# Reading the half-exchanged queries and keys of a rotary embedding by permuted row transfers in place of products with a permutation matrix

## The reference, cut to what matters

```
def rotate(xp, pos):
    half = xp.shape[-1] // 2
    ...
    x1, x2 = jnp.split(xp.astype(jnp.float32), 2, axis=-1)
    return jnp.concatenate([x1 * cos - x2 * sin, x1 * sin + x2 * cos], axis=-1)
rd = HEAD_DIM // 2
return jnp.concatenate([rotate(x[..., :rd], row), rotate(x[..., rd:], col)], axis=-1)
```

## Time and profile before

| | us |
|---|---|
| median of 3 runs | 3360.63 |
| lowest, highest | 3359.15, 3364.89 |
| span of the profiled execution | 3357.8 |
| busy: TensorE, its weight loads | 3114.1 (93%), 2493.0 (74%) |
| busy: VectorE, ScalarE, GpSimd | 1500.2, 1162.7, 831.6 |

### The profile page before, as it was taken

One profiled execution on the slowest core, in us unless ns is written; L12 is line 12 of the kernel. 1 busy time (PEld: TensorE's weight loads), 2 busy tenths in 40 slices (PEclk: granted clock), 3 DMA queues, 4 the chain that ended last, 5 costly groups with the idle time before them and its releaser, 6 DMA issues.

```text
span 3357.8 us, 79208 instructions
## 1 busy us (share of the span) xinstructions
PE 3114.1 (93%) x34382; PEld 2493.0 (74%) x34382; DVE 1500.2 (45%) x2358; ACT 1162.7 (35%) x2403; POOL 831.6 (25%) x518
## 2 busy tenths in 40 slices
PE   7999898999999998999999888989899989989998
PEld 5777676778777786888888666767667667768886
DVE  4455473745444653100144464756565456330033
ACT  4433333423334424211112353434333345342222
POOL 2211111111123132222223221111111243434453
PEclk9999999999999999999999989999999999999999
DMA  5424242434454441111111233413233343522222
GB/s 212 135 97 145 81 142 101 130 121 144 145 166 151 158 169 57 51 63 62 62 50 63 75 101 98 127 63 120 65 122 106 93 140 115 188 69 95 99 88 75
DMA packets 246714, 364.56 MB, mean 109 GB/s; under 512 B 154080, under 2 KB 155376, under 8 KB 245904
## 3 DMA queue, kind: packets, MB, share of 16 engines
q1 hardware_dynamic: 226976, 294.57, 27.6%
q10 hardware_dynamic: 14976, 35.66, 2.7%
q0 software_dynamic: 4464, 29.92, 2.5%
HBM read 290.88 MB, written 69.21 MB: 107 GB/s over the span
## 4 chain that ended last, share of the span: by engine, by line
PE 76%; DVE 6%; issue 5%; ACT 4%; DMA 2%; DVEq 2%; POOLq 2%; PEld 1%; SPq 1%; POOL 0%; PEldq 0%; ACTq 0%
PE banks L281 20%; PE banks L282 18%; PE banks L283 18%; PE banks L1684 2%; PE banks L1023 2%; PE banks L1695 1%; PE banks L1648 1%; PE banks L395 1%; PE banks L1687 1%; PE banks L1745 1%; POOLq L2430 1%; DVE arena L597 1%; PE banks L2057 1%; PE banks L1051 1%; DMA arena<-chunk_inputs 1%
## 5 line engine op out<-in xcount | busy, mean ns | idle before, releaser
L283 PE MATMUL banks<-hx_rounded,slot_rounded 128*128 128x512 f32 (+1 forms) x1624 | 575.1, 354 | 0.0
L906 POOL TENSOR_TENSOR slot_rounded<-slot,branch_weights_high 128x512 fp32r<-128x512 f32 x188 | 251.4, 1357 | 1286.2 <-ACT branch_weights_high L901 1284.9
L281 PE MATMUL banks<-hx_high,weight_parts 128*128 128x512 f32 (+1 forms) x1512 | 537.9, 356 | 10.9 <-DVE hx_low L545 10.4
L281 PE MATMUL banks<-hx_rounded,branch_weights_high 128*128 128x512 f32 (+1 forms) x1280 | 498.8, 390 | 48.1 <-DVE arena L1364 8.6
L282 PE MATMUL banks<-hx_low,weight_parts 128*128 128x512 f32 (+1 forms) x1512 | 538.0, 356 | 0.0
L283 PE MATMUL banks<-hx_high,weight_parts 128*128 128x512 f32 (+1 forms) x1512 | 535.9, 354 | 0.0
L282 PE MATMUL banks<-resid_rounded,branch_weights_high 128*128 128x512 f32 (+1 forms) x1280 | 452.7, 354 | 0.0
L283 PEld LDWEIGHTS banks<-hx_rounded,slot_rounded 128*128 128x128 f32 x1624 | 312.2, 192 | 44.3
L281 PEld LDWEIGHTS banks<-hx_rounded,branch_weights_high 128*128 128x128 f32 x1280 | 245.9, 192 | 128.2 <-issue 75.6
L281 PEld LDWEIGHTS banks<-hx_high,weight_parts 128*128 128x128 f32 x1512 | 286.6, 190 | 55.1 <-issue 14.3
L283 PEld LDWEIGHTS banks<-hx_high,weight_parts 128*128 128x128 f32 x1512 | 286.3, 189 | 41.1
(11 more groups left out here) (263 smaller groups left out, 5853.7 us busy)
## 6 DMA issues: line engine op xcount, KB each, us to landing
slot<-in_w_mix SPq DMA_DIRECT2D x120, 512.0 KB, 3.9
slot<-in_w_ffn_in SPq DMA_DIRECT2D x88, 512.0 KB, 3.3
arena<-chunk_inputs SPq DMA_DIRECT2D x48, 640.0 KB, 4.5
arena<-in_w_ada SPq DMA_DIRECT2D x50, 512.0 KB, 5.1
slot<-in_w_ffn_out SPq DMA_DIRECT2D x44, 512.0 KB, 3.3
slot<-in_w_ada SPq DMA_DIRECT2D x40, 512.0 KB, 4.3
chunk_inputs<-arena SPq DMA_DIRECT2D x80, 256.0 KB, 3.9
arena<-side_projections POOLq DMA_DIRECT2D x16, 1152.0 KB, 6.1
```

Source lines behind the costliest of these rows:

```text
L281: first = nc.tensor.matmul(out, w_hi, x_hi, start=start, stop=False)
L283: return first, nc.tensor.matmul(out, w_lo, x_hi, start=False, stop=stop)
L906: last = nc.gpsimd.tensor_tensor(slots_r[g % 3][:, half], slots[g % 3][:, half], weights_high(g)[:, half], ALU.subtract)
```

## The change

The two products with PERM are taken out. The exchanged queries and keys are read from the DRAM tensor in which they lie anyway, in eight transfers of 16 partitions for each head pair (`load_turned`), each of 32 runs of 2 KB. GpSimd issues them: those of the first head pair at the end of `rwkv_pool`, those of the next head pair after the next pair's `load_qkv`, once the present rotation has been made. VectorE waits for their arrival before the first product with the sines. The semaphore `a_swap` now counts the transposed values alone. The new tile TURNED lies at NORM_AT, in the recurrent stage's working space; the tiles PX, PT and VS, which are laid out after it, move there too.

```diff
@@ rwkv_pool
                     bias_masks(pool, l, 0)
                 tile_rest(pool, l, g)
+            pool.wait_ge(state_pe.sem, state_pe.ready(l, NB - 2, 2))
+            load_turned(pool, 0)
@@ tiles
         RT = [at(SEQ), at(SEQ)]
+        at = Carve(NORM_AT)
+        TURNED = at(2 * SEQ).rearrange("p (j t) -> p j t", j=2)
+        assert at.at <= NORM_AT + 2 * 7 * 2 * CHUNK
         PX = [at(512) for _ in range(2)]
@@ semaphores
-        a_swap = Count(sem("attention_swapped"), HP, 3)
+        a_swap = Count(sem("attention_values_transposed"), HP)
+        turned_loaded = Count(sem("turned_queries_and_keys_loaded"), HP, 16 * 8)
@@ attn_pe
                 pe.wait_ge(a_biased.sem, a_biased.free(l, hp))
-                for j in range(2):
-                    nc.tensor.matmul(bank[j][:, :], PERM, q_of(j, hp), start=True, stop=True).then_inc(a_swap.sem, 1)
                 pe.wait_ge(a_stage.sem, a_stage.ready(l, hp))
@@ attn_act
-                act.wait_ge(a_swap.sem, a_swap.ready(l, hp, 3))
+                act.wait_ge(a_swap.sem, a_swap.ready(l, hp))
@@ attn_dve
-                    dve.wait_ge(a_swap.sem, a_swap.ready(l, hp, j + 1))
-                    nc.vector.scalar_tensor_tensor(out=RT[1], in0=bank[j][:, :], scalar=scale, in1=SIN, op0=ALU.mult, op1=ALU.mult)
+                    if j == 0:
+                        dve.wait_ge(turned_loaded.sem, turned_loaded.ready(l, hp, 16 * 8))
+                    nc.vector.scalar_tensor_tensor(out=RT[1], in0=TURNED[:, j], scalar=scale, in1=SIN, op0=ALU.mult, op1=ALU.mult)
@@ new function
+        def load_turned(pool, hp):
+            for g in range(4):
+                for half in range(2):
+                    to, of = 32 * g + 16 * half, 32 * g + 16 * (1 - half)
+                    pool.dma_start(TURNED[to:to + 16], SIDE[hp, of:of + 16, 3:5, CTX:T]).then_inc(turned_loaded.sem, 16)
@@ attn_pool
                     load_qkv(pool, hp + 1)
+                    pool.wait_ge(a_rot.sem, a_rot.ready(l, hp, 2))
+                    load_turned(pool, hp + 1)
                 for g in range(g0 + (2 if hp else 3), min(g0 + 5, NT)):
```

## The result

The changed kernel takes 3394.82 us at the median of four runs (3388.02 to 3395.86), the kernel before 3359.89 in the same session (3357.71 to 3364.89). The ratio is 1.0098, 95% interval 1.0084 to 1.0111: about 35 us slower, where 3.8 us faster was predicted, and outside the range. The profiled execution has a span of 3393.3 us, 35.5 more than the 3357.8 of before.

What follows compares the result with a forecast made beforehand. TensorE was taken as the bound, busy 93% of the span with 76% of the chain. The terms 2.7-5.2-0.1+3.1-2.2-2.1 gave -3.8 us, from 3360.63 to 3356.8; range 3348 to 3366.

Steps and rivals of the forecast that it cites:

- layer 0, first pair: Layer 0's first head pair: TensorE resumes 2.9 us late, less 1.72, plus about 1.5 for low clock; +2.7 us.
- layer 0, other three: Layer 0's later head pairs: GpSimd's weight rest stays covered despite the issues, so the products' time is gained; -5.2 us.
- layer 1, first: Layer 1's first head pair: staged copies end near 2661.6, transposes began at 2661.75, so the delay is absorbed; -0.1 us.
- layer 1, second: Layer 1's second head pair: issues and slower masks delay GpSimd's rest, TensorE stands 6 us, then low clock; +3.1 us.
- layer 1, third: Layer 1's third head pair: -4.4 us from products, wait and low clock, +2.2 from late rest and slab; -2.2 us.
- layer 1, fourth: Layer 1's fourth head pair: no transfers follow, 1.72 of products and 0.41 of waiting go; -2.1 us.
- issue price: GpSimd's time to issue one new transfer: 0.54 us taken, 0.45 lower end, 0.786 upper; eight are 4.3 us.
- Rival 2: GpSimd's queue becomes the wait, at recurrent stage's end and layer 1's rests: +4.1 us at 0.786 per issue; chance 0.23.
- first head pairs: Start of attention in each layer: ScalarE starts 4.3 us later; +2.7 us in layer 0, -0.1 in layer 1.
- masks: GpSimd's six bias masks beside VectorE's freed rotation, layer 1's second and third pairs: 1.3 us added, near 6.2 for six.
- Rival 3: Full blocking between rotation and masks: masks end 2.9 us late, not 1.3, in two head pairs; sum -0.6, chance 0.12.
- gross gain: TensorE's time for the removed products: 1.72 us per head pair, 13.8 us over the eight, or 0.41%.

Runs made afterwards that it cites:

- e1: Changed kernel without products or transfers, sine products reading unexchanged rows from SBUF; +9.4 us against the kernel before, ratio 1.0024.
- e12: Changed kernel with VectorE waiting before its first sine product for the pair's transposed values; +22.0 us against the kernel before, ratio 1.0060.
- e9: Changed kernel with transfers on SyncE, next pair's masks made within the pair, layer 1's bias loads behind the second tile's slab; 3348.2 us.
- e6: Kernel before with only PX, PT and VS laid where the change puts them, TURNED unused; +0.2 us, ratio 1.0003.
- e10: Kernel before, products kept, with the same reordering of masks and bias loads as e9; 3355.95 us, ratio 0.9986.
- e13: Changed kernel with four of the first head pair's eight transfers issued before GpSimd's arrival and four after; +27.8 us against the kernel before, ratio 1.0082.
- e11: e1 with VectorE waiting before its first sine product for the pair's transposed values; +6.5 us against the kernel before, ratio 1.0010.
- e5: e1 with VectorE waiting for a semaphore TensorE increments where the products stood; +7.6 us against the kernel before, ratio 1.0018.

## Why the prediction was wrong

The parts by the prediction's own terms. Each number is how much later, against the kernel before, VectorE's last copy of a head pair starts than that of the pair before it (for a layer's first pair, than the end of the recurrent stage), from one profiled execution each; the sums were made before rounding.

| term | predicted | changed | e1 neither | e12 held | e9 |
|---|---|---|---|---|---|
| layer 0, first pair | +2.7 | +5.7 | -1.3 | +6.0 | +2.1 |
| layer 0, other three | -5.2 | +4.7 | -1.0 | -0.2 | -0.9 |
| layer 1, first | -0.1 | +7.3 | -1.3 | +5.7 | -0.9 |
| layer 1, second | +3.1 | +6.9 | +4.9 | +2.3 | -2.3 |
| layer 1, third | -2.2 | +4.9 | +2.1 | +2.5 | -5.8 |
| layer 1, fourth | -2.1 | -0.1 | -0.4 | +0.3 | -3.2 |
| sum | -3.8 | +29.4 | +3.1 | +16.6 | -11.1 |

The remaining 6 us of the changed kernel's 35.5 lie in stretches that the change doesn't touch (3.8 before the first seam, 3 in layer 1's recurrent stage, 1 back in the feed-forward part); e6, where only tiles moved, has +1.5, +4.1 and -2.9 in the same three, and nearly the span of before.

**The issue price** was right: 0.54 taken, 0.51 measured. Rival 2, which rested on a dearer issue, is refuted in its price; a queue on GpSimd did cost time, but by another mechanism.

**The first head pairs** failed on a missing term. The delay of ScalarE's start was put at the issues alone, 4.3 us; it was 6.2 and 8.7. The prediction let VectorE alone wait for the landing and never asked whether GpSimd's own drain before the arrival would. In layer 1 the seam was to be absorbed (-0.1); with 8.7 us it is not (+7.3).

**The masks** are the larger error: "I add 1.3" for their slowing in layer 1's second and third pairs, and nothing in layer 0. Measured were 2.9 us in both of these, 2.9, 2.2 and 1.8 in layer 0's later pairs and 1.2 in layer 1's last, which was slow before; and VectorE's rotation became longer as well, 8.6 us in layer 1's second pair against 5.1 in layer 0's first, where it runs alone. The 6.18 of the fourth pair was read as what masks take beside a whole rotation. VectorE's rows of the kernel before in that pair say otherwise:

```profile
2787.37 0.69 DVE L2184 SCALAR_TENSOR_TENSOR arena<-banks,arena 128x512 f32<-128x512 f32 x1 [4.04 <-PE banks L2024]
2788.13 1.88 DVE L2187 TENSOR_TENSOR arena<-arena 128x512 f32<-128x512 f32 x1
2790.14 1.00 DVE L2182 SCALAR_TENSOR_TENSOR arena<-arena 128x512 f32<-128x512 f32 x1
```

The masks began at 2785.70, the products held VectorE until 2787.37, and L2184 read PSUM: in 6.18 us the masks met two operations with both inputs in SBUF, and lost 1.3. In the changed kernel they meet four or five, and lose 2.9. So that row was no upper bound, and what runs beside the masks once the wait is gone should have been drawn up operation by operation. Rival 3 had the mechanism and its size (2.9 late), and failed by its second half: it took late masks for a delay of two rests alone. The rows of the changed kernel and of e1 show two more followers: the bias add, which stands on VectorE behind the masks, and the 32 bias loads, for which the prediction allowed 0.5 us, with slab, ScalarE's L901, exponentials and TensorE behind them. A third is the division L2229, which the prediction did not have at all: it took 4.07 us for two in layer 1's second and third pairs, and TensorE's waits for that line came to 10.9 us in layer 1's attention, against 6.2 before.

On this the Trainium skill, "SBUF — State Buffer", section "Who interferes with whom", states that a VectorE instruction with two SBUF inputs contends with a GpSimd one that reads SBUF. The trace agrees: a mask's median is 854 ns before, 1312 in e1, 866 with VectorE held. The prediction cited that rule and gave it a chance of 0.12.

**The gross gain** of 1.72 us per head pair is real but needs its cover: in e9 against e10 the products' removal is worth 7.8 us of the 13.8.

What the prediction said would be seen: L2024 gone, right; issues at 0.54, right; TensorE's pause behind the seam (4.4 us, not 2 to 3); a wait for GpSimd's rest with a low clock behind it, right in kind (7.27 us, clock 0.50, where 5 to 6 and 0.6 were forecast); masks near 6.2, wrong; no waits for L2190, nearly right (1.3 us in three).

## What to carry to other kernels

A product taken from the bounding engine may be the only thing that keeps two other engines apart. Ask what the consumer does in the time that it used to wait, which engine it then runs beside, and what queues stand behind that one; a stall that "costs nothing" can be a cover. Of transfers put on a queue just before a barrier, count not the issues but the landing of the last: put them where the engine sits idle earlier, or on another engine. And before removing work, try the kernel with neither the old nor the new way (e1): it tells what the change can bring in that order of work, and here it would have shown a loss.

## What the hardware did that was not expected

- GpSimd's drain behind transfers of its own (eight in the changed kernel, four in e13) ended 0.2 to 0.4 us after the last had landed, 2.4 to 4.8 us after its issue, in all four seams looked at.
- In layer 1's second and third head pairs one of VectorE's divisions L2229 (one SBUF input, 128x512) took 3.6 us beside GpSimd's issues and weight rests, where 0.48 is usual. Which of the two held it wasn't tried; with no transfers (e1) the longest is 1.26.
- A rotation operation with two SBUF inputs (L2184 of e11) took 3.61 us beside the issue of a load and two weight rests, and 0.69 in e12 beside the same issue without the rests.
- A semaphore incremented in TensorE's program behind products, with no product to carry it, came so early that VectorE waited for it 0 to 3.1 us, against 3.3 to 6.6 for the products (e5, masks at 7.1 to 7.9 us).
